# Second block: input projections and merge gates as one stage of split products ahead of the two branches, kept in DRAM

## What is computed

```python
h  = modulate(rms_norm_2(x, norm1_w), sh1, sc1)          # 256 tokens
hc = modulate(rms_norm_2(ctx, norm1_w), csh1, csc1)      # 256 context tokens
p  = h @ in_w
pc = hc @ (in_w[:, :A_COLS + B_COLS] if last else in_w)
pa, pb, pg = split_cols(p, [A_COLS, B_COLS, GATE_COLS])
ya, _ = rwkv7_branch(pa, pca, ...)      # 8 units c of two heads: r, k, v
yb, _ = gdn_branch(pb, pcb, ...)        # 8 heads h: q, k, v, z
gate_a, gate_b = jnp.split(jax.nn.sigmoid(pg), 2, axis=-1)
x = x + g1 * ((gate_a * (ya @ up_a) + gate_b * (yb @ up_b)) @ out_w)
x = x + g2 * squared_relu_mlp(modulate(rms_norm_2(x, norm2_w), sh2, sc2), mlp_w1, mlp_w2)
```

## Time and profile before

| | us |
|---|---|
| median of 3 runs | 4611.3 (4608.25 to 4616.4) |
| profiled execution | 4612.11 |
| span of its instructions | 4610.3 |
| TensorE busy | 4130.2 (90%), 37648 matmuls |
| VectorE, ScalarE, GpSimd busy | 1698.2, 1344.8, 1362.0 |
| mean granted TensorE clock | 0.925 |
| HBM | 117 GB/s over the span |

### The profile page before, as it was taken

The page is one execution under the profiler, slowest core; times in us unless marked ns, Lnnn a source line. Parts: engine busy times, 40 slices in busy tenths (PEclk is TensorE's granted clock), DMA queues, the critical chain, the costliest instruction groups (busy, mean ns, idle before and its releaser), DMA issues.

```text
span 4610.3 us, 85155 instructions
## 1 busy us (share of the span) xinstructions
PE 4130.2 (90%) x37648; PEld 3519.6 (76%) x37648; DVE 1698.2 (37%) x3511; ACT 1344.8 (29%) x2395; POOL 1362.0 (30%) x1003
## 2 busy tenths in 40 slices
PE   7998998988989898899868888888879997999998
PEld 5888887888875676676655555555679997999998
DVE  2444434333324444434441333333332234333332
ACT  3343433333431222222121111111122234344442
POOL 2554444444520000000000000000123354666664
PEclk9999988999979999999978889989889997999999
DMA  3344443443431000000003233323034443555553
GB/s 153 141 171 156 168 172 110 173 147 147 147 110 68 32 33 32 32 2 33 32 32 137 110 119 119 120 101 119 28 120 165 178 170 117 185 183 182 184 182 129
DMA packets 74960, 546.49 MB, mean 119 GB/s; under 512 B 8288, under 2 KB 8672, under 8 KB 9824
## 3 DMA queue, kind: packets, MB, share of 16 engines
q1 hardware_dynamic: 74592, 541.03, 32.1%
HBM read 536.80 MB, written 4.19 MB: 117 GB/s over the span
## 4 chain that ended last, share of the span: by engine, by line
PE 79%; DVE 9%; ACT 5%; issue 2%; POOL 2%; DMA 2%; SPq 0%; DVEq 0%; POOLq 0%; ACTq 0%
PE bank L494 78%; DMA wring<-in_w 1%; DVE arena_L L1779 1%; ACT part_L L1164 1%; PE bank L497 1%; POOL smalls L2634 1%; ACT arena_B L1164 1%; POOL part_L L2629 1%; ACT xT L1161 1%; ACT arena_B L1161 0%; DVE part_L L1791 0%; DVE xT L1779 0%; ACT arena_L L1164 0%; ACT xT L1164 0%; ACT arena_L L1310 0%
## 5 line engine op out<-in xcount | busy, mean ns | idle before, releaser
L494 PE MATMUL bank<-act_L,part_L 128*128 128x256 f32 x7296 | 961.4, 292 | 1.9 <-DVE act_L L1796 1.9
L494 PEld LDWEIGHTS bank<-act_L,part_L 128*128 128x128 f32 x7296 | 921.1, 197 | 36.7 <-issue 27.5
L494 PE MATMUL bank<-keep_B,wring 128*128 128x256 f32 (+1 forms) x2432 | 891.4, 507 | 50.4 <-DMA wring<-in_w 39.0
L494 PEld LDWEIGHTS bank<-arena_B 64*64 64x64 f32 (+5 forms) x15488 | 691.4, 146 | 250.2 <-issue 119.9
L494 PE MATMUL bank<-arena_B 64*64 64x64 f32 (+6 forms) x15488 | 824.5, 248 | 58.9 <-DVE arena_B L2175 29.6
L2629 POOL TENSOR_TENSOR part_L<-wring,part_L 128x512 fp32r<-128x512 f32 x304 | 532.0, 1751 | 662.6 <-ACT part_L L1164 662.1
L494 PEld LDWEIGHTS bank<-keep_B,wring 128*128 128x128 f32 x2432 | 459.0, 201 | 311.6 <-issue 200.0
L2629 POOL TENSOR_TENSOR part_M<-wring,part_M 128x512 fp32r<-128x512 f32 x256 | 457.1, 1798 | 307.7 <-ACT part_M L1164 307.7
L1791 DVE TENSOR_TENSOR part_L<-wring,part_L 128x512 fp32r<-128x512 f32 x304 | 219.6, 723 | 516.8 <-ACT part_L L1164 516.8
L1164 ACT ACTIVATE part_L<-wring 128x1024 fp32r<-128x1024 f32 x304 | 320.3, 1054 | 284.9 <-PE bank L494 268.2
L494 PE MATMUL bank<-act_h,part_M 128*128 128x256 f32 x3072 | 381.2, 287 | 22.8 <-DVE act_h L1796 22.8
(11 more groups left out here) (201 smaller groups left out, 3130.3 us busy)
## 6 DMA issues: line engine op xcount, KB each, us to landing
wring<-in_w SPq DMA_DIRECT2D x404, 1024.0 KB, 4.8
arena_B<-in_w SPq DMA_DIRECT2D x64, 1024.0 KB, 4.8
mring<-in_w SPq DMA_DIRECT2D x32, 1024.0 KB, 5.3
arena_B<-in_lora SPq DMA_DIRECT2D x8, 384.0 KB, 3.1
xT<-in_x SPq DMA_DIRECT2D x1, 2048.0 KB, 8.4
x_kept<-xT SPq DMA_DIRECT2D x1, 2048.0 KB, 7.2
arena_B<-in_ctx SPq DMA_DIRECT2D x1, 2048.0 KB, 12.8
xT<-x_kept SPq DMA_DIRECT2D x1, 2048.0 KB, 7.9
```

The costliest lines, as they stand in the source:

```text
L494: return e.matmul(out, lhsT, rhs, start=start, stop=stop)
```

## The change

A new stage P stands between L and B. It computes all input projections of the second block, the 60 that were plain and the 32 gates, as split products with four part buffers, from `B.h`, the split form of h for all 512 tokens (`act_P`). A result goes through `B.zst` to a DRAM tensor `z_kept`; for 256 tokens the two x parts are multiplied by the high weights in one matmul of 512 columns and added afterwards, and the gates go through tanh before they are stored. The 16 modulation groups and their 64 products move from branch B into P. The branches fetch their inputs from `z_kept` with SyncE, a unit ahead, and split each result (ScalarE copy, VectorE subtraction) into `B.y`. The merge multiplies ya and yb as split products, without gate products, with the stored gates fetched from DRAM, and splits each merged sum as it comes. Stage C has four part buffers.

```diff
-NP = {"L": 3, "C": 3, "M": 4}
+NP = {"L": 3, "P": 4, "C": 4, "M": 4}
+PTOK = [512, 512, 256, 256] + [256, 512, 512] * 8 + [256, 512, 512, 256] * 8 + [256] * 32
...
+            def project_p(n):
+                b, u = PJ.take()
+                w.wait_ge(free(PJ, u))
+                for j in range(2):
+                    h = half("P", n, j)
...
+                        if PTOK[n] == 512:
+                            mm(b, wh[:, k, :], x[:, 0, :], start, False)
+                            mm(b, wh[:, k, :], x[:, 1, :], False, False)
+                            t = mm(b, wl[:, k, :], x[:, 0, :], False, stop)
+                        else:
+                            mm(b.rearrange("p (s t) -> p s t", s=2), wh[:, k, :], x[:, :, 0:256], start, False)
+                            t = mm(b[:, 0:256], wl[:, k, :], x[:, 0, 0:256], False, stop)
...
-            weave.run(small_projections())
-            weave.run(branch_a(), feed_a())
+            behind = modulation("P", 8, 24, 4, B.mring, B.sc, B.macc)
+            weave.run(inputs(), behind=behind)
+            weave.run(behind)
+            ends("pe", "P")
+            begins(w, "P")
...
+            weave.run(branch_a())
...
-            behind = modulation_b()
-            weave.run(branch_b(), feed_b(), behind=behind)
-            weave.run(behind)
+            weave.run(branch_b())
...
             def merges():
                 for c in range(16):
-                    yield from project("C", 2 * c, K.act, ("tx",))
-                    yield from project("C", 2 * c + 1, K.act, ("tx",))
...
+                    yield from project("C", c, B.y, ("yl",), apart=True)
...
+            def inputs():
+                for n in range(NPR):
+                    def ev(b, u, n=n):
+                        w.wait_ge(done("zs", n - 4)) if n >= 4 else None
+                        if PTOK[n] == 512:
+                            w.wait_ge(done("pj", "P", n))
+                            cp(B.zst[n % 4], b).then_inc(*mark("act_in", "free", "pj", u))
...
+                        cp(B.zst[n % 4][:, 256:512], b[:, 256:512]).then_inc(*mark("act_in", "zh", n))
+                        if n >= PG:
+                            w.wait_ge(done("zadd", n))
+                            z = B.zst[n % 4][:, 0:256]
+                            af(z, z, ACT.Tanh, scale=0.5).then_inc(*mark("act_in", "ze", n))
...
-                    tt(B.ya[:, c, :], y, b[:, 0:256], mult).then_inc(*mark(V, "free", "d1", u))
-                    counts.at[("ya", c)] = counts.last(V)
+                    tt(y, y, b[:, 0:256], mult).then_inc(*mark(V, "free", "d1", u))
+                    counts.at[("yg", c)] = counts.last(V)
+                    yield
+                    w.wait_ge(done("yh", c))
+                    low(B.y, c, y, "yl", c)
...
+            def put(n):
+                w.wait_ge(done("ze", n))
+                e.dma_start(ZS[n][:, 0:PTOK[n]], B.zst[n % 4][:, 0:PTOK[n]]).then_inc(*mark(f"dma_z{n % 4}", "zs", n))
+
+            def get(n, dst, sem, *event):
+                w.wait_ge(done("zs", n))
+                e.dma_start(dst, ZS[n][:, 0:PTOK[n]]).then_inc(*mark("dma_" + sem, *event))
...
+            for i in range(4):
+                w.wait_ge(done("zrfree", i - 2)) if i >= 2 else None
+                w.wait_ge(done("abt")) if i == 2 else None
+                get(i, D.zr[i % 2][:, 0:PTOK[i]], f"r{i % 2}", "zr", i)
+
+            def load_a(c):
+                for j, key in enumerate("rkv"):
+                    if c == 0:
+                        w.wait_ge(done("zrfree", 2 if key == "k" else 3))
+                    else:
+                        w.wait_ge(done("mixed", key, c - 1))
+                    get(PA + 3 * c + j, D.Z[key], "a" + key, "z", key, c)
```

More of the change, by code:

```diff
@@ L1187, in project @@
                 yield
-            def plain(s, n, step, evac, ring=PJ):
-                b, u = ring.take()
-                for k in range(16):
-                    if k < 15 and k % step == step - 1:
-                        yield
-                w.wait_ge(done("plain", s))
-                evac(b[:, 0:n], u)
-                yield
             def norm(tag, ring, sq, x, ready, rb):
@@ L1809, in project @@
                 yield
-            def plain(s, n, step, ring=PJ):
-                b, u = ring.take()
-                for k in range(16):
-                    if k < 15 and k % step == step - 1:
-                        yield
-                yield
             def norm(tag, ring):
@@ L2644, in project, with modulation @@
                 yield
[L2646 to L2655 removed]
+            def modulation(n0, n1, gap):
+                for n in range(n0, n1):
+                    for _ in range(4 * gap + 8):
                         yield
@@ L2713, in layer_out, with tail @@
                     yield from project("L", 76 * l + n)
-            behind = modulation()
+            def tail(stage, n0, n1):
+                for n in range(n0, n1):
+                    yield from project(stage, n)
+            behind = modulation(0, 8, 15)
             for i in range(4):
@@ L2788, in gpsimd @@
             root(("S", 1), small(1), 2)
+            for h in range(lead("P")):
+                split("P", h)
+            behind = modulation(8, 24, 4)
+            weave.run(tail("P", 0, NPR), behind=behind)
+            weave.run(behind)
+            ends("pool", "P")
+            begins(w, "P")
             w.wait_ge(done("w0h"))
@@ new lines, in inputs @@
+            def inputs():
+                for n in range(NPR):
+                    load(SP + n + NS)
+                    put(n - 2) if n >= 2 else None
+                    for _ in range(4):
+                        yield
+            w.wait_ge(done("hl", 15))
+            w.wait_ge(done("summed", ("S", 1), 3))
+            load_mod(32, B.mring, NMOD)
+            behind = modulation(8, 24, 4, B.mring)
+            weave.run(inputs(), behind=behind)
+            weave.run(behind)
+            put(NPR - 2)
```

599 lines of the change are left out of this document (222 added, 377 removed).

## The result

| | before | after |
|---|---|---|
| median (4 runs each) | 4609.8 us | 4782.5 us (4778.1 to 4785.8) |
| span of the profiled execution | 4610.3 | 4776.3 |
| TensorE busy, matmuls | 4130.2, 37648 | 4020.6, 37936 |

The ratio is 1.037, with a 95% interval of 1.035 to 1.039: 3.7% slower, where 3.1% was predicted. Of the 28 us between 4754 and 4782, 23 are that the span came out longer than forecast; 4.4 lie between the profiled execution and the median, where the forecast had put -1.2.

What follows compares the result with a forecast made beforehand. The kernel looked bound by TensorE, but branch A's projections lay in holes left by VectorE. A gives 36 us, B 338, the merge 217; P costs 788 for 79, its passage 24: 4754 us, range 4705 to 4820.

Steps and rivals of the forecast that it cites:

- The step that decides: Branch A: without projections every unit takes what unit 7 took alone, 119.63 us, plus 0.91 for splitting its result.
- five stretches: Second block before the change: small projections, branch A, branch B, merge and MLP, with TensorE read as 86% to 98% busy.
- 33 x 10.58 + 58 x 5.44: Stage P: projections after the first, 10.58 us each for 512 tokens and 5.44 for 256: 349.1 and 315.5 us.
- A unit of A: Branch A: 120.54 us for each of eight units, 964.3 in all.
- A unit of B: Branch B: 73.9 us for each of eight units, 591.5, after 10.8 us of gate preparation.
- Head, tail, passage, merge and MLP: Remaining terms: P's first projection ends at 1403, its tail 10 us, passage 24.1, merge 7 + 184, MLP 813.3.
- the 9.42 us before the merge: Before the merge: a weight transfer of 9.42 us expected to go, since the first three tiles load during P.
- Rival (a): Branches A and B shrink by what is taken out of them, making the kernel faster: 4406 us; chance 0.04.
- Rival (b): Stage P is bound by transfers, taking 853 us at 211 GB/s: +98, 4852 us; chance 0.10.
- The waiting stores in SyncE's queue: Stage P: a store waiting for an evacuation holds up the next tile's load; costed at nothing.
- Rival (c): TensorE's clock stays low in the branches: +546 us, 5300, if all units fall to 1.2 GHz; a third, 4936; chance 0.05.
- Rival (d): Stage P still makes four passes, 64 and not 48 per projection: +219 us, 4973; chance 0.02.

Runs made afterwards that it cites:

- e1: The kernel before, with the plain projections beside branch A's units 1 to 7 keeping only the last of 16 matmuls: 4584.6 us, 0.9948 of before.
- e5: The changed kernel with unread matmuls of constants in TensorE's holes, 30 per unit of branch A and 13 per unit of B: 4744.3 us.
- e6: The changed kernel with one VectorE multiplication of branch A's preparation issued four times in each direction, six more instructions a unit: 4824.7 us.
- e4: The changed kernel with stage P's 512-token projections in passes of 256 columns, 95 passes where there were 48: 4807.3 us.
- e3: The changed kernel with stage P's products with the low part of the weights left out, transfers and splits kept: 4564.8 us.
- h1: The kernel before, with the merge's first three weight tiles loaded as soon as their buffers are free: 4598.7 us, 0.9979 of before.
- e2: The kernel before, with the plain projections beside branch B's units 0 to 6 keeping only the last of 16 matmuls: 4452.4 us, 0.966 of before.
- h2: The kernel before, with branch A's three weight-tile loads per unit issued ahead of SyncE's wait for the previous unit: 4616.7 us, 1.0018 of before.

## Why the prediction was right, point by point

| | forecast | measured |
|---|---|---|
| first projection of P ends | 1403 | 1406.5 |
| P ends | 2158 | 2186.4 |
| P to the first shift of A | 24.1 | 23.4 |
| branch A, 8 units | 964.3 | 980 |
| branch B with its head | 602.3 | 584 |
| merge | 191 | 190 |
| the rest | 813.8 | 812.8 |
| span | 4753.4 | 4776.3 |

- **The step that decides was right.** The unit that ran alone before is like the seven that run alone now: 119.6 and 0.91 us were forecast, 122.9 came. e1, e5 and e6 show the reason that was given, VectorE's chain with holes in TensorE, for the front part of a unit. The back part is TensorE's own, which the prediction did not see; there the projections cost time (80.8 us for 72.5 at nearly the same clock), and the lone unit's number was right because it held both that gain and what the fallen clock takes of it. The prediction also read TensorE's share of its five stretches as 86% to 98%; the rows give 86% to 96%, and nothing hangs on it.
- **P was mis-sized by the passes**, the term "33 x 10.58 + 58 x 5.44". I took 0.2204 us for 512 columns from a plain product and expected at worst 0.2396. It is 0.230, since a pass has a fixed 12 ns beside its columns (e4); that is 24 us, the largest single error. The time of a plain product's pass is no price for a split one.
- **A unit of A was 2.4 us too short** (122.9 for 120.5, 16 us in all). The back part of unit 7 before took 74.9 us at a clock of 0.90, like the shorter ones of the changed kernel; the longer ones take 78.7 at 0.85, and the mean is 76.7. The front part takes 46.1 us for 44.7, and 0.91 of that is the split. e5 shows that the back part follows the clock. I had put it at 0 to +30 in the range and at 0 in the sum, though its sign was known.
- **A unit of B was 2.2 us too long** (71.7 for 73.9, 18 us with the head), and that is the clock too. Step by step the two units are equal up to the inverse; the 2 us lie in the chain. Here are its 40 matmuls in unit 7 of the kernel before and in a unit of the changed kernel:

```profile
3370.77 10.83 PE L494 MATMUL bank<-arena_B 128*128 128x128 f32 x40 [0.22 <-DVE arena_B L2419]
```

```profile
3541.10 8.81 PE L492 MATMUL bank<-arena_B 128*128 128x128 f32 x40 [0.22 <-DVE arena_B L2335]
```

  The granted clock of the chain was 0.70 there and 0.88 here. One unit is a sample of one phase of the clock, to about 2%: with the same code the units of B take 72.6 to 72.9 us on average in e3, e4 and e6. That A's error (+16 us) and B's (-18) nearly cancel is luck.
- **Head, tail, passage, merge and MLP** were within 4 us each; that the 9.42 us before the merge go is confirmed by h1.
- **Rival (a)** fell to e1. **Rival (b)** did not occur, and e3 shows how far it was: TensorE first waits at 358 GB/s. The waiting stores in SyncE's queue that it rested on took 6.6 us to land and delayed nothing. **Rival (c)** holds in its mechanism at a small part of its price: 2.4 us a unit of A over the forecast, 4.6 over a TensorE that is kept busy, where it had 45. **Rival (d)** did not occur.
- The Trainium skill, same page, section "HAM oscillation — how this bites in real kernels", says that pauses between bursts cost clock; e2 (up to 1.94 us for 1.06) and e5 agree with it.

Left open: why h2's units with projections are over 1 us longer than those of before (127.4 for 125.9), and not equal to them. 1.0 us of it lies in the front part (46.1 for 45.1), where the half clock behind the moved hole is seen; that it is the whole was not tried. Nor was a similar packing of branch B.

## What to carry to other kernels

Before work is moved away from a stage, look for a stretch in which the stage runs without it: its length is what remains, whatever the busy share of the engine says. Work on one engine that lies in holes left by another was free here and cost its full time in a stage of its own; look first whether it can be placed better in the holes before taking it out. And ask what the emptied engine's clock does to the work that stays. And a wait that has the same size as an excess need not be its cause: after removing it, look for what is late next.

## What the hardware showed that I had not expected

- A matmul pass of the split form has a fixed cost of 12 ns beside its columns, 18.7 us over 1551 passes (e4).
- More work on TensorE made the kernel faster: 276 us of busy time added in holes took 38 us off (e5), because the small products behind the holes ran at a higher clock (0.98 to 1.00 for 0.85 to 0.90).
- The same code of branch B took 71.7 us a unit in one run and 72.9 in another, at a granted clock of 0.76 and 0.72 (the changed kernel, e6).
- Weight transfers beside a busy TensorE reached 358 GB/s over 200 us (e3), where 211 was the most that I had read beside a busy TensorE in the kernel before.
- The same modulation group took 1.06 us beside the projections and up to 1.94 without them; the mean of 51 went from 1.12 to 1.51 (e2).
